# Low parts of 16 weight pairs a layer: from a VectorE subtraction to an accumulating DMA

## What is computed

```
h = x * (1.0 + sc1) + sh1
p = h @ w_in[l]
q, k, v, qi, ki, wi, xr, yg = split(p)
rel = relu(einsum('bthd,bsd->bths', qi, ki))
idx_score = einsum('bths,bth->bts', rel, wi)      # causal, then the top 128 of each row
attn_out = attention of q over the chosen k, v    # 4 heads of 128
lru_out = rg_lru(conv(xr)) * gelu(yg)
mix = concat(rms_norm(attn_out), rms_norm(lru_out)) @ w_out[l]
x = layer_norm(alpha * x + (1.0 + g1) * mix)
x = layer_norm(alpha * x + (1.0 + g2) * (square(relu(h2 @ w_up[l])) @ w_down[l]))
```

## Time and profile before

| | |
|---|---|
| median of 3 runs | 1405.91 us (1403.7 to 1410.07) |
| profiled execution | 1405.28 us, of which the span of its trace is 1403.6 us |
| busy in the span | PE 93%, DVE 57%, ACT 39%, POOL 7% |
| granted TensorE clock, mean | 0.958 |
| DMA | 158.56 MB, mean 113 GB/s |

### The profile page before, as it was taken

How to read it: one execution, slowest core, us unless ns; L and a number is a source line. 1 busy time by engine, 2 the same in 40 slices (tenths; PEclk the granted TensorE clock), 3 DMA queues, 4 the chain that set the end, 5 groups by cost and what they waited for, 6 DMA issues and landing times.

```text
span 1403.6 us, 17026 instructions
## 1 busy us (share of the span) xinstructions
PE 1306.1 (93%) x6225; PEld 1024.6 (73%) x6225; DVE 804.7 (57%) x1322; ACT 550.8 (39%) x849; POOL 98.5 (7%) x107
## 2 busy tenths in 40 slices
PE   3999797799999999999999997968999999999996
PEld 2777474577788888888867765647868888888886
DVE  3746779745763634636465557995565344253453
ACT  3833446532731423314346342555355133241331
POOL 3100002002000000000120000010100000000012
PEclk8999998899999999999989998979989999999998
DMA  9753334201235242343245342520213333323221
GB/s 315 242 189 121 105 120 165 91 30 61 76 105 160 94 150 90 104 154 101 75 136 175 126 135 91 179 76 1 90 31 114 100 101 91 104 90 105 90 75 60
DMA packets 73397, 158.56 MB, mean 113 GB/s; under 512 B 6528, under 2 KB 10872, under 8 KB 73336
## 3 DMA queue, kind: packets, MB, share of 16 engines
q1 hardware_dynamic: 59904, 108.61, 24.7%
q0 software_dynamic: 12800, 48.76, 10.4%
q10 hardware_dynamic: 632, 0.39, 0.1%
HBM read 155.64 MB, written 2.10 MB: 112 GB/s over the span
## 4 chain that ended last, share of the span: by engine, by line
PE 80%; DVE 15%; issue 2%; DMA 2%; ACT 1%; POOL 0%; POOLq 0%; DVEq 0%; SPq 0%; ACTq 0%
PE bank L634 23%; PE bank L635 23%; PE bank L636 23%; DVE idx_acc L1594 3%; DVE best L1592 3%; DVE w_lo L1408 2%; PE bank L679 2%; DMA first_mod<-in_w_mod_dram 2%; PE bank L599 1%; PE bank L537 1%; PE bank L852 1%; PE bank L731 1%; PE bank L832 1%; DVE turned_ring L1545 1%; PE bank L889 1%
## 5 line engine op out<-in xcount | busy, mean ns | idle before, releaser
L1408 DVE TENSOR_TENSOR w_lo<-w_raw,w_hi 128x1024 fp32r<-128x1024 f32 (+1 forms) x216 | 236.8, 1112 | 352.7 <-ACT w_hi L968 352.7
L968 ACT ACTIVATE w_hi<-w_raw 128x1024 fp32r<-128x1024 f32 (+1 forms) x216 | 202.7, 959 | 474.6 <-PE bank L636 473.1
L634 PE MATMUL bank<-a_hi,w_hi 128*128 128x512 f32 x896 | 371.4, 415 | 10.9 <-DVE a_lo L1450 7.0
L635 PE MATMUL bank<-a_lo,w_hi 128*128 128x512 f32 x896 | 352.8, 394 | 0.0
L636 PE MATMUL bank<-a_hi,w_lo 128*128 128x512 f32 x896 | 352.7, 394 | 0.0
L634 PEld LDWEIGHTS bank<-a_hi,w_hi 128*128 128x128 f32 x896 | 170.6, 190 | 64.4 <-issue 23.7
L634 PE MATMUL bank<-b_hi,w_hi 128*128 128x512 f32 x512 | 199.7, 390 | 0.0
L635 PEld LDWEIGHTS bank<-a_lo,w_hi 128*128 128x128 f32 x896 | 170.6, 190 | 39.2 <-issue 3.9
L636 PE MATMUL bank<-b_hi,w_lo 128*128 128x512 f32 x512 | 199.2, 389 | 0.0
L635 PE MATMUL bank<-b_lo,w_hi 128*128 128x512 f32 x512 | 199.2, 389 | 0.0
L636 PEld LDWEIGHTS bank<-a_hi,w_lo 128*128 128x128 f32 x896 | 170.3, 190 | 36.5
(11 more groups left out here) (267 smaller groups left out, 1457.3 us busy)
## 6 DMA issues: line engine op xcount, KB each, us to landing
mod_raw<-in_w_mod_dram POOLq DMA_DIRECT2D x40, 1024.0 KB, 6.2
w_raw<-in_w_up_dram SPq DMA_DIRECT2D x64, 512.0 KB, 3.7
w_raw<-in_w_down_dram SPq DMA_DIRECT2D x64, 512.0 KB, 3.7
w_raw<-in_w_in_dram SPq DMA_DIRECT2D x48, 512.0 KB, 4.2
w_raw<-in_w_out_dram SPq DMA_DIRECT2D x16, 512.0 KB, 6.0
first_mod<-in_w_mod_dram SPq DMA_DIRECT2D x4, 1024.0 KB, 19.5
first_mod<-in_w_mod_dram POOLq DMA_DIRECT2D x4, 1024.0 KB, 15.0
x_in<-in_x_dram POOLq DMA_DIRECT2D x4, 512.0 KB, 14.4
```

What stands on the lines that cost most here:

```text
L634: mm(o, wh, hi(kk), start=first, stop=False)
L635: mm(o, wh, lo(kk), start=False, stop=False)
L968: last = af(hi, src, ACT.Copy)
L1408: last = tt(lo, src, hi.bitcast(F32), ALU.subtract)
```

## The change

For the four groups k, q, yg and out0, 16 pairs a layer and 32 in all, VectorE no longer makes the low part. ScalarE writes w_hi as before and then writes w_lo as minus the value of w_raw, rounded to fp32r, which is minus the high part. GpSimd then issues a DMA from w_raw to w_lo whose destination is added to (SBUF to SBUF, 128 x 1024 floats, 512 KB), waits until it has landed, waits for lo_split to stand at the pair before, and adds one to lo_split. The other pairs are split as before.

```diff
--- before.py
+++ after.py
@@ -65,6 +65,8 @@
 RIGHT_ORDER = [1, 2, 3, 0]
 
 MR = 2
+
+DMA_LO = ("k", "q", "yg", "out0")
 
 
 VEC = {}
@@ -272,6 +274,7 @@
         kiwi_in, kiwi_hi_s, kiwi_lo_s = sem("kiwi_in"), sem("kiwi_hi_done"), sem("kiwi_lo_done")
         hi_split, lo_split = sem("hi_split"), sem("lo_split")
         pair_used = sem("pair_used")
+        lo_added = sem("lo_added")
         mod_in = [sem(f"mod_in{s}") for s in range(MR)]
         first_mod_in = [sem(f"first_mod_in{n}") for n in range(NEXT_PAIRS)]
         mods_out = sem("mods_out")
@@ -489,11 +492,28 @@
                         pool.dma_start(blk[64 * par:64 * par + 64, g, :, 64 * par:64 * par + 64],
                                        A[name][l, :, :, :].rearrange("(t two) c d -> two c t d", two=2)[par])\
                             .then_inc(gate_in, 16)
+                def add_raw(name, p):
+
+                    g = group_at(name, l)
+                    n = l * len(DMA_LO) * PAIRS + DMA_LO.index(name) * PAIRS + p
+                    pool.wait_ge(hi_split, g * PAIRS + (p + 1))
+                    pool.dma_start(w_lo[:, p, :, :].bitcast(F32), raw[:, p, :, :], accum_op=ALU.add).then_inc(lo_added, 16)
+                    pool.wait_ge(lo_added, 16 * (n + 1))
+                    pool.wait_ge(lo_split, g * PAIRS + (PAIRS + p))
+                    pool.sem_inc(lo_split, 1)
+
                 for n in range(LATE_PAIRS):
 
+                    if 7 <= n <= 13 and n % 2:
+                        add_raw(DMA_LO[(n - 7) // 2], 3)
                     pool.wait_ge(mod_used, l * MOD_PAIRS + (NEXT_PAIRS + n + 1 - MR))
                     pool.dma_start(mod_raw[:, n % MR, :, :], A["w_mod"][l, :, (MODS_NEXT + 2 * n) * P:(MODS_NEXT + 2 * n + 2) * P]
                                    .rearrange("(k p) n -> p k n", p=P)).then_inc(mod_in[n % MR], 16)
+                    if 5 <= n <= 11 and n % 2:
+                        add_raw(DMA_LO[(n - 5) // 2], 0)
+                        add_raw(DMA_LO[(n - 5) // 2], 1)
+                    if 6 <= n <= 12 and n % 2 == 0:
+                        add_raw(DMA_LO[(n - 6) // 2], 2)
                     if n == LATE_PAIRS - 2:
                         for m in range(LT):
                             pool.wait_ge(decay_done, l * LT + (m + 1))
@@ -964,8 +984,10 @@
                     prev = names[names.index(name) - 1]
                     b = bank_set(prev) + 3
                     act.wait_ge(full_s[b], uses_before(b, f"{prev}3", l, c) + 1)
-                for src, hi, _ in pair_views(name, p):
+                for src, hi, lo in pair_views(name, p):
                     last = af(hi, src, ACT.Copy)
+                    if name in DMA_LO:
+                        last = af(lo, src, ACT.Copy, scale=-1.0)
                 last.then_inc(hi_split, 1)
 
             def a_tile(l, blk, kk):
@@ -1402,7 +1424,11 @@
 
             def split_lo(name, l, p, c=None):
 
+                if name in DMA_LO:
+                    return
                 g = group_at(name, l, c)
+                if name == "out1" and p == 0:
+                    ve.wait_ge(lo_split, g * PAIRS + PAIRS)
                 ve.wait_ge(hi_split, g * PAIRS + (p + 1))
                 for src, hi, lo in pair_views(name, p):
                     last = tt(lo, src, hi.bitcast(F32), ALU.subtract)
```

## The result

| | before | after |
|---|---|---|
| median, us | 1405.93 (1403.7 to 1410.07) | 1461.91 (1461.43 to 1463.06) |
| span of the profiled execution | 1403.6 | 1460.0 |
| mean granted TensorE clock | 0.958 | 0.945 |

The ratio is 1.0396 (95% interval 1.0371 to 1.0421): 56 us slower, 28 a layer, where 10 faster was forecast and 1432 was the upper end of the range.

A forecast was written before the change was run, and what follows sets the result against it. PE, 93% busy, was taken to lose time mainly to VectorE's backlog in the q group. A layer summed to -4.8 - 1.8 + 1.0 + 0.8 = -4.8 us, two layers -9.6, giving 1396 us, range 1391 to 1432.

The forecast's parts named there:

- product of head 4: q group: the indexer product where PE stood for VectorE's backlog, forecast to start at 171.0 us.
- 4.8 and 1.8: q group, us saved a layer: 4.8 from subtractions off VectorE's path, 1.8 from matmuls no longer at the lower clock.
- The clock: PE behind the q group's 8.8 us gap: slow matmuls at 1.2 GHz would vanish, -1.8 us a layer.
- the short one: PE's pause of 0.52 us before the change, which brought no slow matmuls; new pauses, 2.4 us at most, were taken as nearer it.
- the add behind a load: GpSimd's queue: an add issued right behind a modulation load was taken at 7.8 us, against 6.0 for others.
- +0.8 us: yg group: only load 11 would be late for PE, costing 0.8 us a layer.
- The rival: GpSimd's queue becomes the new bound, its chain of adds and loads late in yg; chance 0.36.
- X: Accumulating DMA's time from issue to the sign on lo_split, taken as 6.0 us; break-even at 6.8.
- the out0 adds have 60 us until the attention is over: GpSimd's queue behind yg: out0's adds were given 60 us of slack, with no cost in the sum.
- stay ahead of the exp: GpSimd's queue behind load 14: the recurrence's squares would still come before the attention's exp, with no cost in the sum.
- the other twelve count nothing: VectorE: of a layer's 16 subtractions, the twelve outside q lie beside PE-bound work and gain nothing.
- The +1.0 for the copy behind yg: ScalarE between yg's last split and the attention's first exp: the extra copy delays the exp, +1.0 us a layer.

The follow-up runs named there:

- e1_none: Changed kernel without ScalarE's second copy and without the adding DMA, low parts of the 32 pairs left out: 1392.5 us.
- e2_copy: Changed kernel with ScalarE's second copy but without the adding DMA, so w_raw is not added in: 1392.4 us.
- e9_small: Changed kernel with modulation loads 6 to 13 cut from 1 MB to 128 KB, same order, queue and number of DMAs: 1407.3 us.
- e5_kqyg: Changed kernel with out0's four pairs split by VectorE again; k, q and yg keep the adding DMA: 1425.5 us.
- e12_qout0: Changed kernel with adds for q and out0 only, q's together between loads 8 and 9, out0's behind load 15 and the squares: 1391.2 us.
- e6_qonly: Changed kernel with the adding DMA for q's four pairs alone, same queue places; k, yg and out0 back on VectorE: 1398.1 us.
- e4_sploads: Changed kernel with modulation loads 6 to 13 issued by SP on the hardware queue instead of by GpSimd: 1435.4 us.
- e11_two: Changed kernel with two adds issued at once behind each load, then both waited for: 1410.2 us.

## Why the prediction was wrong

**The gain was read rightly.** VectorE's backlog bound the q group. The product of head 4 was forecast at 171.0 and came at 171.69, in a trace whose late_mod(7) is itself 0.58 later. late_mod(8) came 6.4 us earlier against late_mod(7), where 4.8 and 1.8 make 6.6. ScalarE's k_out was forecast at 156.3 and began at 156.70, and its copies cost nothing (e1_none and e2_copy are equal). The clock was regained as far as the sum needs it. Behind the new pause of 2.25 us matmuls were slow for 2 to 3 us (1.07 us at 160.38; granted clock 0.58 between 161.0 and 163.5), against my reading that it would be like the short one. But in e2_copy no slow matmuls followed a pause of 2.26 us at the same place (granted clock 1.00 from 159.8 to 162.0), and late_mod(8) came equally early in both, 24.82 and 24.81. So the pause alone doesn't decide, and the slow matmuls cost nothing there.

**The step that failed first: the add behind a load, taken at 7.8 us, measured at 11.8.** The first add of two with no load ahead was right (6.0 forecast, 5.8 and 5.1 measured). The second adds from load 8 to load 11, also taken at 6.0, took 7.1, 7.6 and 6.9: the smaller part of the miss. The 7.8 came from two transfers at once in yg, which was the wrong row: there a load met w_raw's transfers, while GpSimd issues its add 0.9 us behind a load every time, with the w_raw load of the sign before beside both. Add and load then take about the sum of what each takes alone (5.8 and 5.8), and the load itself 9.7 instead of 5.8. e9_small shows it by its opposite. The sum had load 11 out at 210.6 and landed at 216.8. GpSimd was through issuing it at 225.5, 14.9 later: the adds behind loads 8, 9 and 10 took 12.1, 11.0 and 12.2 instead of 7.8, which makes 11.9, and the second adds 3.6. It was used at 234.37. The forecast's +0.8 us was +17.7: late_mod(11) came 79.04 us behind late_mod(7), where 67.91 - 6.6 = 61.3 was its time with nothing late. The rival named the right mechanism and signs: GpSimd never idle from q0 to load 11, PE released by landings. Its working has X for one kind of add and X + 1.8 for the other. The two together measured about 18.8 (11.8 and 7.0), so X = (18.8 - 1.8) / 2 = 8.5, and by its 8 us for each us it gives 1433. That is near e5_kqyg (1425.5), not near 1461.9.

**The step that failed second: "the out0 adds have 60 us until the attention is over", and that the squares "stay ahead of the exp".** The adds themselves had the time. But GpSimd's queue is in order, and loads 12 to 14 and the squares stand behind them: the squares began at 265.73, the first exp at 257.10, and the second exp waited 12 us for VectorE, which stood for the squares; I looked at when the adds' results are wanted, not at what stands behind the adds. My own prices would have told it: with load 11 out at 210.6, out0's four adds (7.8 + 6.0, twice, with 0.9 for load 12 between) end at 239.1, and the squares, behind two more loads, start at about 241. Before they started at 235.18, with TensorE 6.4 us later than now. e5_kqyg prices this at 36 us: in the first layer some 9 come between late_mod(11) and (12), whose load stands behind out0's first two adds, and some 10 between (12) and (13), behind the squares. e9_small prices it at up to 15 even with a quick chain. This is what lay outside the range.

**A third step was half right: "the other twelve count nothing".** e12_qout0 leaves k's and yg's subtractions on VectorE and loses nothing by it against e2_copy, so they do count nothing. e6_qonly leaves out0's there too and is 0.5% behind: 1.9 us a layer at late_mod(13) against e2_copy (87.93 and 86.00), the rest later. The two kernels e6_qonly and e12_qout0 also differ in where q's adds stand, but late_mod(12) doesn't show that (71.31 and 72.06). The +1.0 for the copy behind yg shows as 0.9 between late_mod(11) and (12): 10.56 us in e2_copy, 9.61 in e1_none.

**The rule cited.** The Trainium skill's half rate of an adding transfer ("Collectives: The Full Stack", bandwidth ceiling) is stated there for the reduce step of a ring collective. These runs agree with it in direction only: 5.8 us against 3.5 for the plain copy. Adding cost 1.7 us for each 256 KB (5.84 - 4.13), which leaves 2.4 fixed; if the plain copy had the same fixed part, an estimate, its bytes would take 1.1 us against 3.4, and adding would run at a third of the rate, not at half. The Trainium skill's formula in "DMA: Bandwidth & Descriptors", section on one DMA on the software path, gives 3.2 us for the plain 512 KB, near the 3.5, and 4.4 for twice the bytes, below the 5.8. It says nothing of a second transfer beside the first, and that is where the time went.

**What stays open.** The 11.8 us behind a load isn't taken apart fully. A plain copy and a half add behind a load, at 10.7 and 10.8, take longer than the sums of their lone durations with 5.8 (9.3 and 9.9). The w_raw load beside them, which those sums leave out, is a likely reason: in e4_sploads the add without one beside it took 9.2 us, those with one 9.7 to 10.3. No run took it away in the changed kernel's order. How much is the order in one queue and how much the engines is bounded by e4_sploads alone. Why the same pause of 2.25 us at the start of q was followed by slow matmuls in some kernels and not in others is open too.

## What to carry to other kernels

Before work is put on a queue that is in order, list everything that stands behind it there, and when each of those is wanted, not only when the new work is. Here a transfer issued right behind a large one cost about both durations, not its own plus a little, and a wait for each landing in turn adds them all up: issue several, then wait. An offload is worth it where the busy engine is on the path (here q's and out0's pairs, half of those that the change moved), and only there.

## What the runs showed of the hardware

- An accumulating DMA within SBUF, 512 KB of float32: 5.8 us from its issue to the next instruction behind its landing, 4.1 for 256 KB; a plain one of 512 KB 3.5. Right behind a 1 MB load, with a w_raw load of 512 KB beside both, the same three took 11.8, 10.8 and 10.7, and the load 9.7 instead of 5.8.
- The share of busy DMA engines was only 0.62 to 0.67 in these stretches, so the mean share didn't show that a chain of transfers was the bound.
- A GpSimd subtraction of 128 x 1024 took 2.4 us and held up a VectorE product of two tiles for about as long (2.83 instead of 0.68 us), and a mask step of one tile too (1.90 instead of 0.29), but not the topk steps, which also read one. Beside the recurrence's squares on GpSimd, VectorE's product behind them took 2.42 us (changed kernel) and 3.41 (e9_small) instead of 0.68.
- One pause of TensorE of 4.1 us (e1_none) was followed by slow matmuls, where three pauses that sum to the same 4.1 us (2.26, 0.89, 0.95, in e2_copy) cost less: late_mod(8) came 2.3 us earlier, though both kernels end alike. A first pause of 2.25 us was followed by slow matmuls in the changed kernel and e12_qout0, and by none in e2_copy, e9_small and e11_two.
